# The order of the three split products in every wide matrix multiplication of a two-block transformer kernel

## Time and profile before

| what | value |
|---|---|
| median of the three runs | 3778.0 us (3768.46 to 3779.77) |
| the profiled execution, its own time | 3775.43 us |
| its span | 3773.6 us |
| PE multiplications, busy | 15156, 3492.6 us (93% of the span) |
| PE weight loads, busy | 2681.0 us (71%) |
| DVE, ACT, POOL busy | 55%, 17%, 10% |
| mean granted clock of TensorE | 0.937 of 2.4 GHz |

### The profile page before, as it was taken

One profiled execution on the slowest core, in us unless ns is written; L12 is line 12 of the kernel. 1 busy time (PEld: TensorE's weight loads), 2 busy tenths in 40 slices (PEclk: granted clock), 3 DMA queues, 4 the chain that ended last, 5 costly groups with the idle time before them and its releaser, 6 DMA issues.

```text
span 3773.6 us, 45894 instructions
## 1 busy us (share of the span) xinstructions
PE 3492.6 (93%) x15156; PEld 2681.0 (71%) x15156; DVE 2061.4 (55%) x3194; ACT 660.0 (17%) x1354; POOL 391.0 (10%) x292
## 2 busy tenths in 40 slices
PE   6896889998897889998999899999989998989997
PEld 4564468886565468886888676788868886768885
DVE  4555455555556455555544666544555456755446
ACT  2332211111332221111000231200020003320002
POOL 0000130003000140003000243000000003420001
PEclk8997599999997599999999999999999999999998
DMA  4121013222112013222222222223222222222221
GB/s 158 54 65 62 12 59 100 94 96 88 50 62 67 12 49 99 94 97 82 95 95 96 91 70 74 73 95 100 91 78 95 95 92 81 68 67 95 95 96 66
DMA packets 86288, 302.54 MB, mean 80 GB/s; under 512 B 9171, under 2 KB 9939, under 8 KB 85888
## 3 DMA queue, kind: packets, MB, share of 16 engines
q1 hardware_dynamic: 78576, 282.17, 22.7%
q10 hardware_dynamic: 7568, 18.55, 1.5%
HBM read 298.56 MB, written 6.06 MB: 81 GB/s over the span
## 4 chain that ended last, share of the span: by engine, by line
PE 88%; DVE 4%; issue 2%; DVEq 2%; ACT 2%; DMA 1%; POOLq 1%; ACTq 1%; POOL 0%; PEldq 0%; PEld 0%; SPq 0%
PE acc L430 20%; PE acc L432 20%; PE acc L431 20%; PE outp L514 3%; PE acc L480 2%; PE score L526 2%; PE acc L704 2%; PE acc L482 2%; PE acc L481 2%; PE acc L706 2%; PE acc L705 2%; PE trans L501 2%; PE score L466 2%; PE score L597 1%; DVE opL L1313 1%
## 5 line engine op out<-in xcount | busy, mean ns | idle before, releaser
L430 PE MATMUL acc<-opH,wH 128*128 128x512 f32 x2176 | 858.9, 395 | 49.1 <-DVE opL L1313 45.6
L431 PE MATMUL acc<-opL,wH 128*128 128x512 f32 x2176 | 853.5, 392 | 0.0
L432 PE MATMUL acc<-opH,wL 128*128 128x512 f32 x2176 | 852.8, 392 | 0.0
L1303 DVE TENSOR_TENSOR wL<-wraw,wH 128x1024 fp32r<-128x1024 f32 x540 | 732.3, 1356 | 42.0 <-issue 2.1
L1301 DVE CAST wH<-wraw 128x1024 fp32r<-128x1024 f32 x540 | 375.5, 695 | 320.2 <-PE acc L432 270.6
L430 PEld LDWEIGHTS acc<-opH,wH 128*128 128x128 f32 x2176 | 411.8, 189 | 158.9 <-DVE opL L1313 62.5
L432 PEld LDWEIGHTS acc<-opH,wL 128*128 128x128 f32 x2176 | 412.6, 190 | 87.1
L430 PE MATMUL acc<-hidH,wH 128*128 128x512 f32 x1216 | 473.0, 389 | 0.0
L431 PE MATMUL acc<-hidL,wH 128*128 128x512 f32 x1216 | 473.0, 389 | 0.0
L432 PE MATMUL acc<-hidH,wL 128*128 128x512 f32 x1216 | 473.0, 389 | 0.0
L431 PEld LDWEIGHTS acc<-opL,wH 128*128 128x128 f32 x2176 | 413.0, 190 | 83.5
(11 more groups left out here) (234 smaller groups left out, 3587.8 us busy)
## 6 DMA issues: line engine op xcount, KB each, us to landing
wraw<-in_weights SPq DMA_DIRECT2D x508, 512.0 KB, 3.3
wraw<-in_weights SPq DMA_DIRECT2D x32, 384.0 KB, 3.0
big<-bias_scratch ACTq DMA_DIRECT2D x12, 512.0 KB, 3.6
bias_scratch<-bias_rows ACTq DMA_DIRECT2D x3, 1280.0 KB
big<-in_par ACTq DMA_DIRECT2D x2, 1536.0 KB, 7.0
big<-in_x SPq DMA_DIRECT2D x1, 2048.0 KB, 8.7
big<-bias_scratch ACTq DMA_DIRECT2D x2, 1024.0 KB, 5.0
out_x<-big ACTq DMA_DIRECT2D x4, 512.0 KB, 2.6
```

The lines of the kernel that those rows point to most:

```text
L430: pe.matmul(accum[:, :], wH[:, slot, w], hi[:, k, :], start=k == 0, stop=False)
L431: pe.matmul(accum[:, :], wH[:, slot, w], lo[:, k, :], start=False, stop=False)
L432: mm = pe.matmul(accum[:, :], wL[:, slot, w], hi[:, k, :], start=False, stop=k == n - 1)
L1303: dve.tensor_tensor(wL[:, slot, :], wraw[:, slot, :], wH[:, slot, :].bitcast(F32), ALU.subtract).then_inc(split_done, 1)
```

## The change

The three multiplications of a chunk are no longer issued together. A new generator `passes` first runs `wH*opH` and `wL*opH` for all chunks, waiting before each chunk for its high part only (`op_hi`), and then `wH*opL` for all chunks, waiting before each for its low part. `product`, `projection` and `na_piece` all use it. The generators now yield after 8, 16 and 24 multiplications. In `down` the wait stays `hid_ready` in both passes.

```
+            def passes(slot, accum, n, hi, lo, ready):
+
                 for k in range(n):
                     if ready is not None:
-                        pe.wait_ge(*ready(k))
+                        pe.wait_ge(*ready(k, "hi"))
                     w = slice(k * P, (k + 1) * P)
-                    pe.matmul(accum[:, :], wH[:, slot, w], hi[:, k, :], start=k == 0, stop=False)
-                    pe.matmul(accum[:, :], wH[:, slot, w], lo[:, k, :], start=False, stop=False)
-                    mm = pe.matmul(accum[:, :], wL[:, slot, w], hi[:, k, :], start=False, stop=k == n - 1)
+                    pe.matmul(accum, wH[:, slot, w], hi[:, k, :], start=k == 0, stop=False)
+                    mm = pe.matmul(accum, wL[:, slot, w], hi[:, k, :], start=False, stop=False)
+                    if k in (3, n - 1):
+                        yield mm
+                for k in range(n):
+                    if ready is not None:
+                        pe.wait_ge(*ready(k, "lo"))
+                    mm = pe.matmul(accum, wH[:, slot, k * P:(k + 1) * P], lo[:, k, :], start=False, stop=k == n - 1)
+                yield mm
+
+            def product(slot, rnd, accum, n=NC, hi=opH, lo=opL, ready=None):
+
+                pe.wait_ge(split_done, rnd * SLOTS + slot + 1)
+                for turn in passes(slot, accum[:, :], n, hi, lo, ready):
+                    mm = turn
                 mm.then_inc(pieces_done, 1)
...
-                         (lambda k: (hid_ready, hids + k + 1)) if r == 0 else None)
+                         (lambda k, part: (hid_ready, hids + k + 1)) if r == 0 else None)
...
-                return lambda k: ((op_lo, op_lo_pool)[k % 2], n * (NC // 2) + (k // 2 + 1))
+                def ready(k, part):
+                    if part == "hi":
+                        return op_hi, n * NC + (k + 1)
+                    return (op_lo, op_lo_pool)[k % 2], n * (NC // 2) + (k // 2 + 1)
+
+                return ready
...
-                    for k in range(NC):
-                        if ready is not None and j == 0:
-                            pe.wait_ge(*ready(k))
...
-                        if k == NC - 1:
+                    for n, mm in enumerate(passes(j, acc[j % 2][:, :], NC, opH, opL, ready if j == 0 else None)):
+                        if n == 2:
                             mm.then_inc(pieces_done, 1)
-                        if k in (2, 5, NC - 1):
-                            yield
+                        yield
```

More of the change, by code:

```diff
@@ L422, in _ @@
         def _(pe):
+            def passes(slot, accum, n, hi, lo, ready):
+                for k in range(n):
+                    if ready is not None:
+                        pe.wait_ge(*ready(k, "hi"))
+                    w = slice(k * P, (k + 1) * P)
+                    pe.matmul(accum, wH[:, slot, w], hi[:, k, :], start=k == 0, stop=False)
+                    mm = pe.matmul(accum, wL[:, slot, w], hi[:, k, :], start=False, stop=False)
+                    if k in (3, n - 1):
+                        yield mm
+                for k in range(n):
+                    if ready is not None:
+                        pe.wait_ge(*ready(k, "lo"))
+                    mm = pe.matmul(accum, wH[:, slot, k * P:(k + 1) * P], lo[:, k, :], start=False, stop=k == n - 1)
+                yield mm
             def product(slot, rnd, accum, n=NC, hi=opH, lo=opL, ready=None):
                 pe.wait_ge(split_done, rnd * SLOTS + slot + 1)
-                for k in range(n):
-                    if ready is not None:
-                        pe.wait_ge(*ready(k))
-                    w = slice(k * P, (k + 1) * P)
-                    pe.matmul(accum[:, :], wH[:, slot, w], hi[:, k, :], start=k == 0, stop=False)
-                    pe.matmul(accum[:, :], wH[:, slot, w], lo[:, k, :], start=False, stop=False)
-                    mm = pe.matmul(accum[:, :], wL[:, slot, w], hi[:, k, :], start=False, stop=k == n - 1)
+                for turn in passes(slot, accum[:, :], n, hi, lo, ready):
+                    mm = turn
                 mm.then_inc(pieces_done, 1)
@@ L698, in na_piece @@
                 pe.wait_ge(split_done, layer * (ROUNDS2 * SLOTS) + ((ROUND_B2 + ROUND_NA) * SLOTS + n + 1))
[L699 to L707, removed]
+                for turn, mm in enumerate(passes(n % SLOTS, acc[n % 2][:, :], NC, opH, opL, ready)):
+                    if turn == 2:
                         mm.then_inc(pieces_done, 1)
-                    if k in (2, 5, NC - 1):
-                        yield
+                    yield
             def na_turn_values(layer, pair):
```

## The result

| | before | after |
|---|---|---|
| median of the runs on the same chip | 3777.49 us (3768.46 to 3779.77, 6 runs) | 3791.93 us (3789.58 to 3796.73, 6 runs) |
| ratio | | 1.0044, 95% interval 1.0031 to 1.0057 |
| profiled execution, its span | 3773.6 us | 3788.2 us |
| mean granted clock | 0.937 | 0.929 |
| PE multiplications | 15156, 3492.6 us busy | 15156, 3523.7 us busy |

The change made the kernel slower, by 14 us between the medians, against a forecast of 12 (3790, with 3774 to 3802 as its range). The count of multiplications is the same; PE is busy for 31 us more. The mean granted clock fell from 0.937 to 0.929, which is some 475 us of the span at 1.2 GHz before and some 538 after; 63 us more at 0.47 each come to about 30, an estimate that fits the 31.

What follows compares the result with a forecast made beforehand. PE was taken to bound the kernel (88% of the chain), with its low clock mattering more than its waits. Terms 9.5 + 0.1 - 3.1 + 5.4 = +11.9 us gave 3787.3 for the profiled execution, 3790 median; range 3774 to 3802.

Steps and rivals of the forecast that it cites:

- The forecast case: Whole kernel: the terms sum to +11.9 us, 3790 on the median; chance 0.48.
- Behind rmsnorms: Five first products: ten multiplications behind the last high part, clock rising 3.7 us later; 1.9 us each, +9.5 us.
- my 0.15 for a full clock: Products behind rmsnorms: even at full clock each ends 0.15 us later, 0.8 us in all.
- Behind layer norms: Five first products: 4.3 us gain at full clock, against 0.9 us clock delay each, 4.4 in all; +0.1 us.
- Out projections: Four products: one multiplication instead of three behind GpSimd's last low part; -1.1 and -0.5 us, twice each, -3.1 us.
- Down products: First down products: last hidden chunk wanted earlier; 0.55 us eight times, 0.26 four times, nothing in eight others; +5.4 us.
- What I cost at nothing: Changed generator yields, weight slots coming free and additional met waits: no cost, at most some tenths from the yields.
- The new yields: Generators yielding after 8/8/8 instead of 9/9/6: at most some tenths move, covered by PE's own backlog.
- Met waits: Eight more waits in each product that has any: met in nearly all cases, counted as no cost.
- Rival C: Low pass: met waits keep weight loads from running ahead, 0.11 us each; 512 waits add 56 us, 3846; chance 0.07.
- A: Ten products behind normalizations: the clock is up anyway, so not slower; -1.2 us, 3777; chance 0.28.
- B: Attention cores: one twentieth more or less low-clock time, 11 us either way, 3779 or 3801; chance 0.17.

Runs made afterwards that it cites:

- the second two profiles: The kernel before and the changed kernel, each profiled once more with nothing changed: 3773.4 and 3795.2 us, one execution each.
- the fill: Changed kernel plus, in four first products' high pass, a third multiplication per chunk but the last, into an unread bank: 3775.8 us, ratio 1.0020.
- the skewed order: Kernel before, but waiting first products issue a chunk's two high-part multiplications, then the previous chunk's low-part one: 3766.7 us, ratio 0.9989; again 3766.2, 0.9979.

## Why the prediction was right, point by point

**The sum.** Forecast +11.9; measured +14.4 between the medians (the ratio's interval is +12 to +22 us), +14.6 between the first two profiles, of which 13.4 lie in the terms. The forecast case was the one that came. That it came so close is partly luck: between the second two profiles the difference is +21.9, of which 17.5 lie in the terms, and 4.4 outside.

**Behind rmsnorms**, forecast +9.5, measured +8.1 and +9.0, plus 0.9 and 1.8 for the low clock that reached into the next product. The mechanism stands: the end hangs on the last chunk, ten multiplications stand behind it, and they run at the low clock. I had taken a delay of 3.7 us from the last high part to the clock's rise; in the four that lost in the first profile it was between 3.4 and 6.0 us, so the average was too low, by some 0.7 us; and I had all five lose where four did. The two errors nearly cancel in the first pair. One of the five did not lose: behind the second layer's attention rmsnorm PE began 3.4 us after the fixed point instead of 2.1 to 2.2, in the kernel before just as late. By then high parts lay ready, it ran ten multiplications without a gap, the clock rose, and the product ended 0.2 us later than before, which is my 0.15 for a full clock. The second profile of the changed kernel shows the same. A late start is no guarantee. With the down products put back, PE began at this place just as late and also ran ten multiplications without a gap, and yet the clock was low again for the last ones; the product took 15.63 us, 1.6 more (that kernel, start to next product):

```profile
911.14 0.79 PE L454 MATMUL acc<-opH,wH 128*128 128x512 f32 x1 [4.21 <-ACT opH L903]
...
919.37 0.50 PE L454 MATMUL acc<-opH,wH 128*128 128x512 f32 x1 [1.55 <-ACT opH L903]
919.71 0.55 PE L455 MATMUL acc<-opH,wL 128*128 128x512 f32 x1
920.05 3.46 PE L461 MATMUL acc<-opL,wH 128*128 128x512 f32 x8
923.35 0.39 PE L454 MATMUL acc<-opH,wH 128*128 128x512 f32 x1
```

What held PE back there, and a later start made on purpose, were not tried.

**Behind layer norms**, forecast +0.1, measured +1.6 and +3.2, inside the bounds of -4.3 and +4.4. The size was off: I gave this denser pass half of the rmsnorm's delay on the mean of five. In these two profiles a product has the full loss or none: at the low clock to the end 4.0 to 4.3 us behind the last high part, in the other case 2.45, and the first was the more common, three and five of five. The half had no row behind it; it was a guess. In the kernel before, too, it changes from one profile to the next which of these products lose (two of five, then three). One row was misread: the window 3143.57:3155.68 ends at the second multiplication triple of the next product (x27, where the others have 25), so the kernel before took 0.7 us less there than I counted (11.43 us, not 12.11). That made the change look 0.7 us better than it is; counted rightly the term is +0.8.

**Out projections**, forecast -3.1, measured -3.2 and -2.5. The only gain in the sum. (The second is less because the kernel before did one of the four 0.6 us faster in its second profile.) It is there because GpSimd's low parts, 1.6 us each, come last whatever PE does, and one multiplication instead of three stands behind the last. The timeline of the changed kernel, the last low multiplication and the next product:

```profile
496.27 0.50 PE L436 MATMUL acc<-opL,wH 128*128 128x512 f32 x1 [0.63 <-POOL opL L1879]
496.60 0.39 PE L429 MATMUL acc<-opH,wH 128*128 128x512 f32 x1
```

496.60 is 8.06 us after the first high part; it was 9.13 before.

**Down products**, forecast +5.4 (0.55 and 0.26 each), measured 0.60 and 0.30, +6.0. The chunk came when the rows said, and was wanted when the new order said:

```profile
600.36 0.69 DVE L1714 TENSOR_TENSOR hidL<-big,hidH 128x512 fp32r<-128x512 f32 x1
600.44 0.39 PE L430 MATMUL acc<-hidH,wL 128*128 128x512 f32 x1
...
601.11 0.50 PE L429 MATMUL acc<-hidH,wH 128*128 128x512 f32 x1 [0.28 <-DVE hidL L1714]
601.45 0.39 PE L430 MATMUL acc<-hidH,wL 128*128 128x512 f32 x1
```

Wanted at 600.66, given at 601.11, and 0.34 instead of 0.23 us to the next. The idle time printed in the row (0.28) is less than the loss, since a multiplication's own end is counted 0.16 us past its successor's normal start. The eight parts of eight chunks in the second block cost nothing, as forecast.

**What I cost at nothing.** The new yields: nothing in the stages' lengths. The neighbourhood stage took 147.9 us in the changed kernel from its first product on, 148.06 before. Met waits: with the down products put back, the first network's stretch took 351.20 us, and 350.5 when the 0.7 us of low clock at its start are taken off; before 350.49. Sixteen waits in each of seven products stand in it. Rival C is out.

**Rivals.** A (the clock is up anyway) happened at three of ten places in one profile and at one in the other; the fill made it happen at three more. B (the clock moves in the attention cores) is real in size, 14 us between profiles, but shows no side clear of that scatter: +2.3 and +5.0 us in the pairs, both layers together. In this kernel two multiplications a chunk left the windows at 0.50 to 0.52 in seven of ten places of the first profile, and at 0.69 to 0.86 in the other three; three a chunk gave 0.73 to 0.76 in the filled ones. The rule of the Trainium skill's page "TensorE: Matmul & The Clock Gate", section "Loop structure matters more than you think", that the loop nest decides whether matmuls stay warm, agrees with these windows; the section's own example is a long wait for a DMA, which is not the wait here.

## What to carry to other kernels

An order that starts work on the first half-operand that is ready helps only if little is left to do when the last one arrives; count the instructions behind the last arrival, not the time of the first. Sparser work in front of a dense part can cost more through TensorE's clock than the idle time it fills. The same order applied where both halves arrive together can only lose or break even (twelve of the twenty first down products lost, eight broke even), so put it where its wait is: here the out projections, and elsewhere the skewed order.

## What the runs showed of the hardware that I had not expected

- Extra multiplications made a product end sooner: 31 in 11.0 to 12.0 us against 24 in 12.7 to 13.9 us at the same three places, at a granted clock of 0.73 to 0.76 instead of 0.50 to 0.52.
- The first block's attention took 413 to 427 us over nine profiles, with PE's granted clock between 0.82 and 0.85, and 416 to 427 us in the two profiles of one kernel. With 1559 multiplications each time it can only be seen by comparing several profiles; one pair of profiles can be off by 10 us in its total while its first products repeat within some hundredths.
- A first multiplication after a wait took 0.60 us to the next one at the low clock (554.18 to 554.78) and 0.34 at the full one: 0.17 and 0.11 us more than in a gapless row. I put it down to the weight load: in the trace the load starts together with that multiplication, while in a gapless row it starts with the multiplication before.
